# A layer starts with its first q and k group instead of its first convolution pair, and the norm's factors are turned inside the third unit

## What is computed

```
for layer in range(2):
    h = rmsnorm(x, mix_norm_gain)                  # x * rsqrt(mean(x^2) + eps) * gain
    proj = h @ w_in                                # 1024 -> 3*512 + 2*512
    q, k, v, conv_in = split(proj)
    q, k = rope(rmsnorm per head(q)), rope(rmsnorm per head(k))
    attn = dilated_attention(q, k, v)
    a, g = split(conv_in)
    u = causal_dwconv(a * sigmoid(g))              # 31 taps, 512 channels
    u = silu(layernorm(u))
    x = x + concat(attn, u) @ w_out
    x = x + gated_conv_ffn(rmsnorm(x))             # 3 taps, hidden width 2816
```

## Time and profile before

| | us |
|---|---|
| median of 3 runs | 2506.35 |
| the runs | 2504.84, 2506.35, 2508.18 |
| the profiled execution | 2505.93 |
| its span, from the first to the last instruction | 2504.1 |
| mean granted clock of TensorE | 0.988 of full speed |
| layer 0: input projection from its first matmul to the first attention step on DVE | 11.0 to 271.5 |
| layer 1: the same | 1258.5 to 1514.4 |

### The profile page before, as it was taken

One profiled execution on the slowest core, in us unless ns is written; L12 is line 12 of the kernel. 1 busy time (PEld: TensorE's weight loads), 2 busy tenths in 40 slices (PEclk: granted clock), 3 DMA queues, 4 the chain that ended last, 5 costly groups with the idle time before them and its releaser, 6 DMA issues.

```text
span 2504.1 us, 31220 instructions
## 1 busy us (share of the span) xinstructions
PE 2439.3 (97%) x11696; PEld 2025.8 (81%) x11696; DVE 1588.4 (63%) x1509; ACT 793.4 (32%) x1050; POOL 134.1 (5%) x56
## 2 busy tenths in 40 slices
PE   7999899999999999999999998999999999999998
PEld 6888798878888888888778887987888888888887
DVE  5889885456555555555649898846565555555555
ACT  4222565332222222222232226644322222222221
POOL 0121001010000000000102210011000000000000
PEclk9999999999999999999999999999999999999999
DMA  3223630111111111111112245401111111111111
GB/s 134 76 76 97 188 95 25 51 42 51 51 50 42 50 50 42 50 50 42 42 34 76 75 131 152 114 9 42 51 43 51 50 50 50 44 48 50 49 43 75
DMA packets 46380, 159.35 MB, mean 64 GB/s; under 512 B 7392, under 2 KB 7776, under 8 KB 46304
## 3 DMA queue, kind: packets, MB, share of 16 engines
q1 hardware_dynamic: 45728, 156.22, 20.5%
q10 hardware_dynamic: 576, 2.10, 0.2%
HBM read 133.12 MB, written 25.17 MB: 63 GB/s over the span
## 4 chain that ended last, share of the span: by engine, by line
PE 76%; DVE 14%; DVEq 5%; issue 3%; ACT 2%; DMA 0%; SPq 0%; ACTq 0%; POOLq 0%
PE mm L399 47%; PE aux L399 19%; DVE y L1056 6%; PE aux L566 4%; PE mm L530 3%; PE aux L550 2%; DVEq L1058 2%; DVE w_lo L992 1%; DVE x_lo L1004 1%; DVE sc L1187 1%; DVE y L1220 1%; DVEq L1093 1%; DVEq L999 0%; PE aux L423 0%; DVEq L1102 0%
## 5 line engine op out<-in xcount | busy, mean ns | idle before, releaser
L399 PE MATMUL mm<-x_hi,w_hi 128*128 128x512 f32 x2304 | 724.0, 396 | 31.2 <-DVE x_lo L1004 11.5
L399 PE MATMUL mm<-x_lo,w_hi 128*128 128x512 f32 x2304 | 717.2, 393 | 0.0
L399 PE MATMUL mm<-x_hi,w_lo 128*128 128x512 f32 x2304 | 716.8, 392 | 0.0
L399 PEld LDWEIGHTS mm<-x_hi,w_hi 128*128 128x128 f32 x2304 | 432.8, 189 | 127.7 <-issue 30.8
L399 PEld LDWEIGHTS mm<-x_lo,w_hi 128*128 128x128 f32 x2304 | 436.5, 189 | 95.3
L399 PEld LDWEIGHTS mm<-x_hi,w_lo 128*128 128x128 f32 x2304 | 436.0, 189 | 93.6
L695 ACT ACTIVATE w_hi<-w_raw 128x1024 fp32r<-128x1024 f32 x188 | 197.0, 1058 | 770.4 <-PE mm L399 576.0
L998 DVE TENSOR_TENSOR x<-x,aux 128x1024 f32<-128x1024 f32 x176 | 214.8, 1220 | 127.9 <-PE aux L399 118.3
L992 DVE TENSOR_TENSOR w_lo<-w_raw,w_hi 128x1024 fp32r<-128x1024 f32 x188 | 229.7, 1229 | 35.6 <-ACT w_hi L695 24.4
L1056 DVE SCALAR_TENSOR_TENSOR y<-u_pad,cpar,y (+1 forms) x152 | 208.1, 1369 | 22.9 <-issue 19.4
L1010 DVE TENSOR_TENSOR uv<-mm,rinv 128x1024 f32<-128x1024 f32 x44 | 53.9, 1224 | 223.8 <-PE mm L399 223.6
(11 more groups left out here) (158 smaller groups left out, 2357.5 us busy)
## 6 DMA issues: line engine op xcount, KB each, us to landing
w_raw<-weights SPq DMA_DIRECT2D x188, 512.0 KB, 3.5
qk_scratch<-m SPq DMA_DIRECT2D x64, 128.0 KB, 2.1
qk_scratch<-o SPq DMA_DIRECT2D x64, 128.0 KB, 2.1
x_hi<-qk_scratch SPq DMA_DIRECT2D x32, 256.0 KB, 5.7
q_first<-qk_scratch SPq DMA_DIRECT2D x8, 512.0 KB, 3.5
k_hh_first<-qk_scratch SPq DMA_DIRECT2D x16, 256.0 KB, 5.6
k_ll_first<-qk_scratch SPq DMA_DIRECT2D x16, 256.0 KB, 6.1
x_lo<-v_scratch SPq DMA_DIRECT2D x8, 512.0 KB, 6.8
```

The lines of the kernel that those rows point to most:

```text
L399: last = pe.matmul(acc[:, cols], a, b[:, cols], start=start and n == 0, stop=stop and n == 2)
```

## The change

Units 0 and 1 of a layer become the two halves of the first q and k group, and units 2 and 3 the first convolution pair; `_columns` orders the weights in the same way. The other units keep their places. In `first_units` the last two k steps are no longer interleaved, so unit 0 ends before unit 1's last two k steps. The eight transposes of the norm's factors no longer stand between unit 1 and unit 2 but in the middle of unit 2, after its fourth k step. They read `o2`, since `sb_` now holds a square by then, and the angles of the rotation lie in `o1` instead of `tg`.

ACT now begins with the copies of unit 0, its w_hi of unit 2, `widen`, the copies of unit 1, its w_hi of unit 3 and `read_rinv`. DVE begins with the w_lo tiles of units 2 and 3, in layer 0 the angles, and then reads units 2 and 3.

```diff
-                    order += [(u, k) for k in range(lead, KT) for u in range(2)]
+                    order += [(u, k) for k in range(lead, KT - 2) for u in range(2)]
+                    order += [(u, k) for u in range(2) for k in (KT - 2, KT - 1)]
...
                 first_units()
-                spread(sb_, 0, 0)
-                unit(0, 0, U_QK, U_QK)
+                unit(0, 0, 2, 2, midway=lambda: spread(o2, 0, 0))
                 if l == 0:
                     rope_tables()
-                unit(1, 1, U_QK + 1, U_QK + 1)
+                unit(1, 1, 3, 3)
...
                 small_mean(TB, 0, D_MODEL)
-                unit_done(0)
-                hi(0, 2)
-                widen(sb_, 1, 0)
+                qk_read(0, 0)
+                widen(o2, 1, 0)
+                qk_read(1, 0)
                 read_rinv(0)
-                unit_done(1)
-                hi(1, 3)
                 if l == 0:
                     act.wait_ge(rope_reduced, 1)
...
                 act.wait_ge(params_loaded, 16 * N_PARAMS)
+                unit_done(2)
+                hi(0, 4)
+                unit_done(3)
+                hi(1, 5)
                 conv_gate(0)
                 conv_first_tap(0)
-                qk_read(0, 2)
-                qk_read(1, 2)
...
+                qk_read(0)
+                if l == 0:
+                    rope_angles()
                 dve.wait_ge(statb_read, at(l, STAT_B, 2))
                 dve.memset(u_pad[:, :, 0:TAPS - 1], 0.0)
                 dve.wait_ge(params_loaded, 16 * N_PARAMS)
-                lo(0, 2)
-                scaled(u_pad[:, 0, TAPS - 1:], 0, 0)
-                if l == 0:
-                    rope_angles()
-                conv_gate(0, 1)
+                conv_value(0, 2)
+                conv_gate(0, 3)
                 conv_gated(0)
                 dve.wait_ge(conv_first, at(l, CT, 1))
-                qk_read(2, between=lambda: taps(0, TAPS_OWN))
+                taps(0, TAPS_OWN)
                 if l == 0:
                     dve.wait_ge(rope_full, 1)
                     dve.tensor_copy(sin[:], stat_b[:]).then_inc(rope_ready, 1)
                     dve.tensor_copy(cos[:], stat_s[:]).then_inc(rope_ready, 1)
```

More of the change, by code:

```diff
@@ L57 @@
 GROUPS = FT // 2
-U_CONV, U_QK, U_V = 0, 2, 2 * CT + 2 * QKG
+U_V = 2 * CT + 2 * QKG
 U_OUT = U_V + PAIRS
@@ L174, in trunk @@
         rope_angle, rope_turns = m4[:, 0:SEQ // HPT], m4[:, SEQ // HPT:2 * SEQ // HPT]
-        rope_s, rope_c = tg[:, 0:SEQ // HPT], tg[:, SEQ // HPT:2 * SEQ // HPT]
+        rope_s, rope_c = o1[:, 0:SEQ // HPT], o1[:, SEQ // HPT:2 * SEQ // HPT]
         rope_pos = m2[:, 0:SEQ // HPT]
@@ L1078, in qk_read @@
                 def qk_read(mbase, i=0, between=None):
-                    dve.wait_ge(qk_copied, at(l, 2 * QKG, mbase // 2, 2, i))
+                    copies = 1 if mbase == 0 else mbase // 2
+                    dve.wait_ge(qk_copied, at(l, 2 * QKG, copies, 2, i))
                     dve.sem_inc(mm_read, 1)
                     lo(0, mbase + 2, 4, i)
-                    between()
-                    dve.wait_ge(qk_copied, at(l, 2 * QKG, mbase // 2 + 1, 2, i))
+                    if between:
+                        between()
+                    dve.wait_ge(qk_copied, at(l, 2 * QKG, copies + 1, 2, i))
                     dve.sem_inc(mm_read, 1)
@@ L1397, in _columns @@
     for c in range(CT):
-        units += [np.arange(P) + 3 * ATTN + c * P, np.arange(P) + 3 * ATTN + CONV_CH + c * P]
+        conv = [np.arange(P) + 3 * ATTN + c * P, np.arange(P) + 3 * ATTN + CONV_CH + c * P]
         which, grp = divmod(c, HEADS // HPT)
@@ L1402, in _columns @@
                                          for h in range(HPT)]))
+        units[-2:] = units[-2:] + conv if c == 0 else conv + units[-2:]
     for t in range(PAIRS):
```

## The result

The changed kernel takes 2520.46 us (median of 6 runs, 2517.18 to 2521.70) against 2506.36 for the kernel before beside it (6 runs): ratio 1.0056, 95% interval 1.0043 to 1.0069, 14.1 us slower. The forecast was 2522.0 in a range of 2516 to 2528, and slower. The profiled execution of the changed kernel took 2519.4 with a span of 2517.6, 13.5 more than the span before.

What follows compares the result with a forecast made beforehand. The prediction took DVE, a closed chain of work from loop entry to attention, as the bound. Layer 0's 9.5 us plus layer 1's 6.2 gave 15.7 over the profiled 2505.93, with 0.42 for the median 2522.0, range 2516 to 2528.

Steps and rivals of the forecast that it cites:

- whatever PE gains ahead of it is given back in waits: Ahead of DVE's loop entry, any time PE gains returns as waits; the removed gap's 3 to 4 us bring nothing.
- Layer 0, the entry: DVE enters its loop in layer 0 at 91.2 instead of 81.73, costing 9.5 us.
- The sines: In layer 0, the rotation's sines are done at 56.7, PE waits for them, and unit 3 starts at 60.0.
- the lower clock on unit 3: Layer 0 bound: PE's wait for the sines brings unit 3 the lower clock, 1.9 us more (11.4).
- DVE is not held by PE: Layer 0: after its 8.7 us wait PE is +6.8 to +8.7, no later than DVE's +9.5.
- 5.2 + c: Layer 1's later loop entry; c is unit 2's lower-clock cost after a 1.6 us wait, 0 to 1.9, taken as 1.0.
- The sum: Layer 0's 9.5 plus layer 1's 6.2 make 15.7 us; the terms' ends give 13.2 to 18.5.
- Rival (b): Faster: table copies don't hold PE at the sums after unit 4, being done by 82.0; 2500.2 us, chance 0.03.
- Rival (c): The gap isn't filled: unit 2 starts as late as before, up to 4.0 us more in layer 1; 2526, chance 0.05.
- Rival (e): POOL's power or sum meets the first 8 taps, taking 12.77 instead of 10.82, at most twice; 2525.9, chance 0.07.
- a further drain: Estimate by the skill page: ACT's table load ends 1.4 us later in each layer, sum 18.5 instead of 15.7.
- Rival (d): ACT's table load starts only once the preceding w_hi copy has fully left ACT, twice 1.29 us; 2524.6, chance 0.08.

Runs made afterwards that it cites:

- b1: Kernel before the change, with DVE's first taps and rotation-table copies moved ahead of its w_lo tiles of units 4 and 5; ratio 1.0008.
- b2: e1 and b1 together, plus the angles ahead of the read of unit 0 and two late taps moved before the loop; 2492.8 us against 2501.47, ratio 0.9964.
- d1: Kernel before the change, with seven extra DVE instructions ahead of DVE's loop in layer 0; ratio 1.0044.
- after_again: The changed kernel run once more, unedited, beside new runs of the kernel before; 2523.07 us against 2501.47, ratio 1.0081.
- c1: The changed kernel, with DVE's two rotation-table copies moved ahead of the scaled gate, into DVE's wait for unit 3; ratio 1.0071 to the kernel before.
- c2: c1, and besides the rotation's angles moved ahead of DVE's first w_lo tile, into its wait for the norm; ratio 1.0039 to the kernel before.
- e1: Kernel before the change, unit order kept, gap at unit 2 shortened by earlier norm sums (layer 0), transposes and reordered ACT and DVE steps; ratio 0.9987.
- l1_only: The change applied in layer 1 alone, layer 0 keeping the order of the kernel before; ratio 1.0017 to the kernel before.

## Why the prediction was right, and where its steps were off

- **The bound.** That a later entry of DVE into the loop delays attention by as much held: 189.8 to 191.2 us between the two marks in the eight kernels other than b1 and b2, with entries from 80 to 92, and d1 shows it with nothing else changed. b1 (192.4) and b2 (191.3 with two taps fewer in between) are the ones in which DVE comes early and waits for PE. Whether PE's gain alone is always given back ("whatever PE gains ahead of it is given back in waits") wasn't tried by itself, since every edit that moves PE here moves DVE too; b1 shows that DVE alone gains nothing either.
- **Layer 0, the entry.** 91.2 forecast, 91.11 measured, by two steps whose errors cancel, and that is luck. The sines were done at 54.9 instead of 56.7, since everything from the norm's sums on ran about 1.5 earlier. But after PE's wait of 2.19 for them the table products ran at the lower clock and took 5.06 (54.96 to 60.02) instead of 3.27. I had put the lower clock on unit 3, as a bound, and not on these products. In the repetition it stayed away, the products took 3.37 and the entry was at 89.69, 1.5 before the forecast.
- **Layer 0, PE against DVE.** "DVE is not held by PE" was wrong by 1.3 us. The step that failed is the size of the lower clock after the long wait: I allowed up to 1.9, from unit 2's 1.93 in the earlier trace rows. The sums took 3.43 instead of 1.70 (94.26 after 90.83; before 85.66 after 83.96), and unit 5 13.60 instead of 10.98, 4.3 in all. Attention was therefore 10.8 later, not 9.5.
- **Layer 1.** 5.2 + c, with c taken as 1.0. Measured 5.2 at the entry, and c was 0: after waits of 1.51 and 1.49 in the two executions unit 2 ran at the full clock. To attention it was 5.5. In after_again, c1 and c2 it was 6.7 to 6.9 at the entry, by the slow pairs behind the norm's sums and not by the wait that c stands for.
- **The sum.** 10.8 and 5.5 are 16.3 at the two attention steps, against 15.7 forecast. The profiled execution ended only 13.5 later, because stretches that the change doesn't touch differed: 1.5 more between the first attention step and layer 1, 4.3 less behind the attention of layer 1. The medians differ by 14.1, and by 20 in the second comparison. The size of the forecast is right within what one comparison can tell.
- **The rest.** Rival (b), the faster one, fell where it was said to be decided: the copies were done at 90.6 instead of by 82.0. Rival (c) didn't occur, unit 2 started 5.5 earlier. Rival (e) didn't either: the first 8 taps took 10.81 and 10.87. For the table load the trace speaks against a further drain: in the changed kernel a w_hi copy ends at 72.4, the load starts at 72.42, and the sigmoid at 73.71. The Trainium skill, page "ScalarE: Activation LUTs", section "What ACT_TABLE_LOAD costs", would have 1.38 us more between them. Rival (d) falls with it. ACT at this place:

```profile
71.34 1.06 ACT L695 ACTIVATE w_hi<-w_raw 128x1024 fp32r<-128x1024 f32 x1 [15.48 <-PE mm L399]
72.42 1.28 ACT L746 ACT_TABLE_LOAD   x1
73.71 1.06 ACT L746 ACTIVATE o<-o 128x1024 f32<-128x1024 f32 x1
```

## What to carry to other kernels

A gap on the busiest engine is worth filling only if the engine behind it doesn't pay: list what the other engine did in the meantime and ask when its own long work can now begin. A wait that appears downstream, here 8.6 us for a copy, may only show a lag that was made earlier; removing it moved the wait to the next w_lo tile. Where two engines are in balance, an edit that advances one alone can give nothing (b1, for DVE), and the gain comes from advancing both (e1 and b2). And a forecast that is met to 0.1 us in one trace should be read in a second one: here two steps were off by 1.8 us each and cancelled.

## What the runs showed of the hardware

**The scatter of single executions comes in part from the clock in stretches that no edit touches.** Between the start of the layer norm's centring in layer 1 and the end, the span was 837.5 to 837.7 us in five of the ten traces (before, c1, c2, b1, e1), 834.4 to 834.6 in three (changed, d1, l1_only), and 836.0 and 840.5 in b2 and after_again. For the kernel before and the changed one the difference lies half in the last 22 us of the output projection and half in the last 30 us of the program. Windows of the first place, first of the kernel before, then of the changed one. The columns are the stretch, its length, the busy time of PE, PEld, DVE, ACT and POOL (with the number of instructions), the granted clock, the DMA engines' share and GB/s:

```profile
1740.00:1762.40 22.40, 19.86 (x81) 16.00 (x80) 13.24 (x9) 8.44 (x9) 8.90 (x3) 0.92 0.15 46
```

```profile
1755.00:1777.50 22.50, 19.96 (x89) 16.21 (x88) 14.92 (x11) 10.12 (x11) 8.91 (x3) 1.00 0.15 47
```

In 22.50 us the changed kernel got through 89 matmuls where the one before got through 81 in 22.40, at a granted clock of 1.00 instead of 0.92. PE waits once in each, for the same thing and as long. Before the change the pairs behind this wait ran at half rate for a while:

```profile
1749.63 0.81 PE L399 MATMUL mm<-x_hi,w_hi 128*128 128x512 f32 x2 [2.54 <-DVE x L998]
...
1751.09 1.06 PE L399 MATMUL mm<-x_hi,w_lo 128*128 128x512 f32 x2
```

In the changed kernel they didn't:

```profile
1766.27 0.70 PE L399 MATMUL mm<-x_hi,w_hi 128*128 128x512 f32 x2 [2.54 <-DVE x L998]
...
1767.27 0.62 PE L399 MATMUL mm<-x_hi,w_lo 128*128 128x512 f32 x2
```

At the second place the wait is of 2.75 us in both, and again only the kernel before ran slow after it. Each of the two costs 1.6 us. A wait of 2.5 and one of 2.7 us stand in each layer of all ten traces, 40 in all; the lower clock followed 26 of them and stayed away after 14. After neither of the two in layer 0 did it come in e1 and b2, which is 3.2 of the 4.6 us named under e1. What decides is open; it wasn't tried. It does set what a comparison of single traces can tell: some 3 us in each layer, the size of one of this kernel's edits.

**Which waits cost the clock.** In the projections and the feed-forward part no wait of 1.0 to 1.7 us was followed by slow pairs (1.05 instead of 0.62), in over fifty cases of the ten traces. One of 1.87 (e1) was. Of three waits for the sines of 2.2 us, one was (changed) and two weren't (after_again, c1). From 3.7 us on, all were. The price varied more than I had taken: 1.8 us on the table products after 2.19, 1.9 on unit 2 after 3.69, and 4.3 after 8.65.
